# Masking the keys instead of the values in the state update of an mLSTM decode kernel

## The reference

```
ws = exp(src - m_new)                       # a weight for each token
decay = exp(b_last + m - m_new)
C_new = decay * C + einsum('bsh,bshv,bshk->bhvk', ws, vb, kb)
```

## Time and profile before

| | |
|---|---|
| median of 3 runs | 1560.38 us (1559.88 to 1560.7) |
| profiled execution, first to last instruction (span) | 1558.1 us |
| profiled execution, whole time | not on the page; the median of the runs is 2.3 us above the span |
| PE busy | 1529.1 us, 98% |
| DVE busy | 890.9 us, 57% |
| ACT busy | 659.0 us, 42% |

### The profile page before, as it was taken

How to read it: one execution, slowest core, us unless ns; L and a number is a source line. 1 busy time by engine, 2 the same in 40 slices (tenths; PEclk the granted TensorE clock), 3 DMA queues, 4 the chain that set the end, 5 groups by cost and what they waited for, 6 DMA issues and landing times.

```text
span 1558.1 us, 30694 instructions
## 1 busy us (share of the span) xinstructions
PE 1529.1 (98%) x11365; PEld 1497.8 (96%) x11365; DVE 890.9 (57%) x1522; ACT 659.0 (42%) x928; POOL 78.8 (5%) x142
## 2 busy tenths in 40 slices
PE   6999999999999999999999999999999999999996
PEld 5999999999999999999999999999999999999996
DVE  5655565554443447676666666676667644444443
ACT  5433333333333334454545454544544434343442
POOL 3000000000000000101000000101010000000000
PEclk9999999999999999999999999999999999999998
DMA  6674655556555554564747374747465555555543
GB/s 185 211 172 136 174 150 170 159 163 217 162 162 164 168 155 141 164 215 129 234 122 249 113 260 116 244 124 243 129 208 163 182 162 162 166 165 172 181 155 135
DMA packets 233137, 268.03 MB, mean 172 GB/s; under 512 B 8656, under 2 KB 221848, under 8 KB 232112
## 3 DMA queue, kind: packets, MB, share of 16 engines
q1 hardware_dynamic: 221472, 226.36, 48.5%
q0 software_dynamic: 11632, 41.22, 7.6%
HBM read 244.48 MB, written 23.06 MB: 172 GB/s over the span
## 4 chain that ended last, share of the span: by engine, by line
PE 92%; issue 5%; DVE 1%; DMA 1%; ACT 0%; POOL 0%; DVEq 0%; SPq 0%; POOLq 0%; ACTq 0%
PE ps L394 27%; PE ps L395 27%; PE ps L396 27%; PE ps L561 2%; PE ps L549 2%; PE ps L573 1%; PE ps L694 1%; PE ps L623 1%; PE ps L518 1%; DMA xt<-in_x_sample_dram 1%; PE ps L423 0%; DVE otok L1481 0%; PE ps L520 0%; PE ps L684 0%; PE ps L658 0%
## 5 line engine op out<-in xcount | busy, mean ns | idle before, releaser
L989 DVE TENSOR_TENSOR wlo<-raw,whi 128x1024 fp32r<-128x1024 f32 x416 | 508.2, 1224 | 577.8 <-ACT whi L746 574.7
L394 PE MATMUL ps<-xh,whi 128*128 128x288 f32 x2560 | 768.3, 300 | 0.0
L746 ACT ACTIVATE whi<-raw 128x1024 fp32r<-128x1024 f32 x416 | 440.2, 1059 | 766.5 <-PE ps L396 752.4
L396 PE MATMUL ps<-xh,wlo 128*128 128x288 f32 x2560 | 757.0, 296 | 0.0
L395 PE MATMUL ps<-xl,whi 128*128 128x288 f32 x2560 | 756.9, 296 | 0.0
L394 PEld LDWEIGHTS ps<-xh,whi 128*128 128x128 f32 x2560 | 482.0, 188 | 3.5 <-issue 1.2
L395 PEld LDWEIGHTS ps<-xl,whi 128*128 128x128 f32 x2560 | 482.5, 188 | 0.2
L396 PEld LDWEIGHTS ps<-xh,wlo 128*128 128x128 f32 x2560 | 481.9, 188 | 0.0
L394 PE MATMUL ps<-yh,whi 128*128 128x288 f32 x512 | 151.9, 297 | 0.0
L395 PE MATMUL ps<-yl,whi 128*128 128x288 f32 x512 | 151.4, 296 | 0.0
L396 PE MATMUL ps<-yh,wlo 128*128 128x288 f32 x512 | 151.3, 296 | 0.0
(11 more groups left out here) (308 smaller groups left out, 1146.0 us busy)
## 6 DMA issues: line engine op xcount, KB each, us to landing
raw<-in_w_in_dram SPq DMA_DIRECT2D x320, 512.0 KB, 3.7
raw<-in_w_pb_dram SPq DMA_DIRECT2D x32, 512.0 KB, 3.5
Cin<-in_state_mlstm_C_dram POOLq DMA_DIRECT2D x16, 1024.0 KB, 8.5
out_dram<-Cin POOLq DMA_DIRECT2D x16, 1024.0 KB, 6.2
raw<-in_w_pa_dram SPq DMA_DIRECT2D x32, 512.0 KB, 3.5
raw<-in_w_out_dram SPq DMA_DIRECT2D x32, 512.0 KB, 3.5
xt<-in_x_prompt_dram SPq DMA_DIRECT2D x2, 1024.0 KB, 6.1
out_dram<-cpo POOLq DMA_DIRECT2D x8, 256.0 KB, 2.4
```

The costliest lines, as they stand in the source:

```text
L394: nc.tensor.matmul(out, whi[:, c, kk, cols], mh_[:, k, :], start=(k == 0), stop=False)
L396: last = nc.tensor.matmul(out, wlo[:, c, kk, cols], mh_[:, k, :], start=False, stop=(k == KT - 1))
L746: nc.scalar.activation(whi[:, c], raw[:, c], ACT.Copy).then_inc(hi_ready, 1)
L989: nc.vector.tensor_tensor(wlo[:, c], raw[:, c], whi[:, c].bitcast(F32), ALU.subtract).then_inc(lo_ready, 1)
```

## The change

The mask goes to the other operand. `of_sequence` writes masked keys, `km[:, b % 4]`, from `kst`; `vst` is the stationary operand for all sequences, every second column for each half. `new_states(h, q)` handles the pair of sequences 2q and 2q+1: two matmuls, one for each half of the values, each with the masked keys of both sequences as 512 moving columns, into bank 2 for the first half and bank 3 for the second. Each pair uses the same two banks, so from q = 1 on it waits until both `add_state` of the pair before are done; it also waits for both masks at its start. `cs_mm` counts pairs instead of sequences. `add_state` reads its two halves from two banks. Bank 5 is no longer used by the update, and the wait for it ahead of line 694 goes.

```diff
--- before.py
+++ after.py
@@ -51,7 +51,7 @@
 Y_PARTS = ([(P, 0, slice(c, c + D // 4)) for c in (0, D // 4)] + [(P, 0, slice(D // 2, D))]
            + [(P, 1, slice(c, c + D // 2)) for c in (0, D // 2)] + [(S, 2, slice(0, D))])
 LO = 32
-NEW_BANK = (2, 3, 5)
+NEW_BANK = 2
 EPS = 1e-6
 MASKED = -30000.0
 NEVER = -3.0e38
@@ -205,7 +205,7 @@
     qk = a("qk", [P, 4, T])
 
 
-    vm = nc.alloc_sbuf_tensor_at("vm", [P, 4, XPW], F32R, offset=a.at)[:, :, 4:4 + DH]
+    km = nc.alloc_sbuf_tensor_at("km", [P, 4, XPW], F32R, offset=a.at)[:, :, 4:4 + DH]
     xp = a("xp", [P, 4, XPW])
     kv4 = a("kv4", [P, 2, 2, P])
     hb = a("hb", [P, 3, DH])
@@ -289,9 +289,9 @@
     kt_t, kt_ev, kvs_t, kvs_ev, vt_t, vt_ev, num_mm, den_step, r_set, sq_set, var_set, rs_set, f_set = (
         sem(n) for n in ("kt_t", "kt_ev", "kvs_t", "kvs_ev", "vt_t", "vt_ev", "num_mm", "den_step", "r_set",
                          "sq_set", "var_set", "rs_set", "f_set"))
-    h_set, ht_t, z_set, gate_set, yf_set, ya_hi, cp_mm, cp_ev, nn_ev, vm_set, cs_mm, cs_ev = (
+    h_set, ht_t, z_set, gate_set, yf_set, ya_hi, cp_mm, cp_ev, nn_ev, km_set, cs_mm, cs_ev = (
         sem(n) for n in ("h_set", "ht_t", "z_set", "gate_set", "yf_set", "ya_hi", "cp_mm", "cp_ev",
-                         "nn_ev", "vm_set", "cs_mm", "cs_ev"))
+                         "nn_ev", "km_set", "cs_mm", "cs_ev"))
     q_step, ct_lo, lo_rows = sem("q_step"), sem("ct_lo"), sem("lo_rows")
     inter_mm = sem("inter_mm")
     ya_lo, st_lo, kv4_set = sem("ya_lo"), sem("st_lo"), sem("kv4_set")
@@ -564,14 +564,14 @@
                                             skip_group_check=True)
             last.then_inc(inter_mm, 1)
 
-        def new_state(h, b):
-
-            pe.wait_ge(vm_set, 8 * h + b + 1)
-            if b >= 3:
-                pe.wait_ge(cs_ev, 8 * h + b - 2)
+        def new_states(h, q):
+
+            pe.wait_ge(km_set, 8 * h + 2 * q + 2)
+            if q >= 1:
+                pe.wait_ge(cs_ev, 8 * h + 2 * q)
             for vh in range(2):
-                last = nc.tensor.matmul(ps[:, NEW_BANK[b % 3], DH * vh:DH * vh + DH],
-                                        vm[:, b % 4, vh::2], kst[:], start=True, stop=True)
+                last = nc.tensor.matmul(ps[:, NEW_BANK + vh, :], vst[:, vh::2],
+                                        km[:, 2 * (q % 2):2 * (q % 2) + 2, :], start=True, stop=True)
             last.then_inc(cs_mm, 1)
 
         with pe.Fori(0, HEADS) as h:
@@ -659,8 +659,7 @@
                                                 vz[:, j, P * t:P * t + P], ident[:])
                     last.then_inc(vt_t, 1)
                     pe.wait_ge(slot_free[1], H_USE[1] + 2 + 2 * h)
-                    for b in range(2):
-                        new_state(h, b)
+                    new_states(h, 0)
                 if c == 1:
 
                     pe.wait_ge(lo_rows, h + 1)
@@ -672,11 +671,9 @@
 
                     nc.tensor.matmul(ps[0:S, X4, 0:DH + 1], W[0:2 * S, 384:416], vtok_h[0:2 * S, 2, :],
                                      start=False, stop=True, skip_group_check=True).then_inc(num_mm, 1)
-                    for b in range(2, 4):
-                        new_state(h, b)
+                    new_states(h, 1)
                 if c == 2:
-                    for b in range(4, 6):
-                        new_state(h, b)
+                    new_states(h, 2)
                 if c == 3:
                     pe.wait_ge(h_set, h + 1)
                     for j in range(2):
@@ -685,10 +682,7 @@
                         last = pe.transpose(ps[:, X6 + j, TP:T], hb[0:S, 2, P * j:P * j + P],
                                             ident[0:S, 0:S])
                     last.then_inc(ht_t, 1)
-                    for b in range(6, NB):
-                        new_state(h, b)
-
-                    pe.wait_ge(cs_ev, 8 * h + 6)
+                    new_states(h, 3)
                     for vh in range(2):
                         for t in range(2):
                             last = nc.tensor.matmul(ps[:, X5, DH * vh:DH * vh + DH], vtok_h[:, t, vh:DH:2],
@@ -1257,14 +1251,14 @@
 
         def of_sequence(h, b):
             if b >= 4:
-                dve.wait_ge(cs_mm, 8 * h + b - 3)
-            nc.vector.tensor_scalar(vm[:, b % 4, :], vst[:].bitcast(F32), mask8[:, b:b + 1], None,
-                                    ALU.mult).then_inc(vm_set, 1)
+                dve.wait_ge(cs_mm, 4 * h + b // 2 - 1)
+            nc.vector.tensor_scalar(km[:, b % 4, :], kst[:].bitcast(F32), mask8[:, b:b + 1], None,
+                                    ALU.mult).then_inc(km_set, 1)
 
         def add_state(h, b):
-            dve.wait_ge(cs_mm, 8 * h + b + 1)
+            dve.wait_ge(cs_mm, 4 * h + b // 2 + 1)
             nc.vector.scalar_tensor_tensor(Cin[:, b], Cin[:, b], dec_bc[:, ds(8 * h + b, 1)],
-                                           ps[:, NEW_BANK[b % 3], :].rearrange("p (v k) -> p v k", v=2),
+                                           ps[:, NEW_BANK:NEW_BANK + 2, DH * (b % 2):DH * (b % 2) + DH],
                                            ALU.mult, ALU.add).then_inc(cs_ev, 1)
 
         with dve.Fori(0, HEADS) as h:
```

## The result

The changed kernel takes 1564.12 us (median of 10 runs, 1563.27 to 1564.63) against 1559.97 for the one before (10 runs, 1559.41 to 1560.7): ratio 1.0026, 95% interval 1.0017 to 1.0035. It is 4.15 us slower. Forecast: 1563.4, range 1559.3 to 1565.0, that is +3.0 us with bounds of +1.2 and +3.8 for the two holds (a hold is a place where PE stands idle at a wait). The time lies in the range; the increase is just over the upper bound of its own sum. On the forecast's own base of 1560.4 it would be 1564.5, in the range too.

What follows compares the result with a forecast made beforehand. PE, 98% busy, was taken to bound the kernel. Per head 0.21 + 0.21 - 0.04 = 0.38 us, over 8 heads +3.0, took the span from 1558.1 to 1561.1; with 2.3 more, 1563.4 us, range 1559.3 to 1565.0.

Steps and rivals of the forecast that it cites:

- Pair 0's hold: At each head's first pair, PE waits for both masks instead of one: 0.21 us later, 0.10 to 0.25.
- Pair 2's hold: At the third pair, PE waits for the add_state of sequence 3: 0.21 us late, 0.10 to 0.25.
- pair 1's gain: At the second pair no wait holds; it gains 0.04 us, which is only waited at pair 2.
- The wide matmul: In new_states, two matmuls of 512 columns replace four of 256: 443 ns a pair for 480, 37 ns less.
- p: Pitch of one wide fp32r matmul on PE: 216 to 227 ns, taken as 222.
- d + l: At a hold, DVE's end to weight load (0.10 us) plus load to first column (0.11 us).
- DVE, roles, banks: Masked keys, swapped operands and add_state reading two PSUM banks were claimed to cost nothing.
- Nothing takes the delay back: After each hold, PE waits nowhere for something that doesn't itself start from PE, so the delay stays.
- (a): Rival: weights go in ahead of the held matmul, so l vanishes from both holds; +1.3 us, 1561.7; chance 0.12.
- (b): Rival: only one hold binds, pair 0 or pair 2 alone; +0.7 to +1.0 us, 1561.3; chance 0.10.
- (c): Rival: neither hold binds, -1.2 us, 1559.2, or a far cheaper wide matmul; chance 0.09, of which 0.03 the latter.
- (d): Rival: a wide fp32r matmul takes as long as plain fp32, 432 ns; +13 us, 1577; chance with other slowing 0.06.

Runs made afterwards that it cites:

- e3: The changed kernel with pair 0 as four matmuls of 256 columns, each sequence waiting for its own mask alone: 1562.22 us against 1559.78, ratio 1.0016.
- e1: The changed kernel, same waits and banks, but each pair as four matmuls of 256 columns instead of two of 512: 1564.3 us against 1559.78, ratio 1.0030.
- e4: The changed kernel with the add_state of sequence 3 right behind that of sequence 2, all pairs wide: 1561.81 us against 1559.78, ratio 1.0013.
- e2: The kernel before with only the roles swapped, masked keys moving and values stationary, one sequence at a time: 1560.09 us against 1559.78, ratio 1.0003.
- e5: The changed kernel with the edits of e3 and e4 together: 1560.09 us against 1559.85, ratio 0.9999.
- e7: e6 with each wide matmul issued twice, 64 more in all: 1574.42 us, 14.37 over e6.
- e6: The changed kernel, all pairs wide, add_state 3 early, pair 0 moved behind the first six matmuls of chunk 1: 1560.05 us against 1559.85, ratio 1.0001.
- e10: The kernel before with only the v transposes moved to bank 6, not waiting for st_lo: 1559.83 us against 1559.93, ratio 1.0001.

## Why the prediction was right, step by step

- **Pair 0's hold:** forecast 0.21 (0.10 to 0.25), measured 0.26. Shown by e3, which takes it away, and e1, which keeps it without the wide matmul. The distance from mask to load (d) was 0.11 for the 0.10 taken. The prediction took the old load at 1048.22 for one that ran on without waiting. It stood 1048.22 - (1047.76 + 0.35) = 0.11 behind the end of the first mask, the distance of a load that a wait just released, and so it does in all eight heads (0.12). The new load stands at the same distance behind the second mask. So the hold is the 0.27 between two masks less the 0.01 that the wide pair gains, whatever d and l are.
- **Pair 2's hold:** forecast 0.21, measured 0.28 behind L394 of pair 1; with pair 1's gain, 0.27. d was 0.12. The load was 0.17 ahead of the end of `add_state` 3 and is 0.12 behind it: 0.29, less 0.01. Shown by e4. As forecast, pair 1's 0.01 is only waited there.
- **The wide matmul:** the mis-sized term. Forecast p 222 ns (216 to 227), measured 235 in the chain and 232 over seven heads, outside the bounds. It is in every pair: 2 x 0.013 at each hold, and pairs 1 and 3 gain 0.01 in place of 0.04. For the upper bound I had taken the 13 ns beside the 107 of 256 columns as a cost of each instruction. By the chain most of it grows with the columns: 120 ns for 256 is 0.47 ns a column, a chunk's (1058.20 - 1054.54 - 0.48)/24 = 133 ns for 288 is 0.46, and 235 for 512 is 0.46. So joining matmuls saves only about 0.01 us a pair (0.47 for 0.48 in the chain; 0.04 a head between e1 and the changed kernel).
- **d + l:** with p = 0.235 the stretch from mask to L394, 1052.52 - 1051.82 = 0.70, leaves 0.23 for d + l, 0.21 taken. All the sizes are off to the same side; the sum, 0.38 a head, came out at 0.52, 3.0 us at 4.2.
- **DVE, roles, banks:** costed at nothing. e2 shows about 0.3 us for the roles, the 744 ns of `add_state` for the two banks.
- **Nothing takes the delay back:** right; e5 and the 0.53 a head.
- **Rivals:** (a) weights ahead of the held matmul: against it the after trace, the loads at 1051.93 and 1061.59 come 0.11 and 0.12 behind the releaser and not before. The pulling of weight loads ahead of matmuls in flight that the Trainium skill's page "TensorE: Matmul & The Clock Gate" (Step-by-step: what each phase is for) states does not reach over a wait here. (b) one hold: both are there. (c) neither, or a far cheaper wide matmul: e7. (d) a wide matmul as slow as plain fp32: e7.
- **The chances:** slower by over 0.2% had 0.38, same 0.59; the measured 0.26% is over that bound, though its interval begins at 0.17%, below it. The forecast stood 0.1 us under the bound, and the mis-sized terms decided the side.

## What to carry to other kernels

When matmuls are joined into wider ones, look at what the wide one must wait for: the last input of all its parts, and all the room that it writes. Here each join gained 0.01 us and two of four cost over 0.25 us on a PE that is busy 98% of the time. And before the number of instructions is counted as a saving, take the cost for each column at two widths: if it is the same, there is nothing per instruction to save. Holds hang on small margins: the old loads came 0.16 (pair 0) and 0.17 us (pair 2) before the end of the input that the new ones wait for, and that decided this change. Moving the producer's step (e4) or the consumer (e6) by one place gave it back.

## What the runs showed of the hardware

- A fp32r matmul of 512 columns takes 235 ns at the granted 2.4 GHz in a stream (e7's chain), and not the 512/2.4 = 213 of its columns; one of the two records of a plain fp32 matmul of 256 columns takes 216. Why fp32r costs more for each column stays open.
- The load of a held matmul starts 0.12 us behind the end of the DVE instruction that releases it, in all eight heads within 0.01 (pairs 0 and 2 after, e10's first mask; L658 before). The first column is an estimated 0.12 later, from the 0.23 for d + l above: a hold costs about 0.23 us beyond the releaser's end even when it is missed by little.
- A wait that ends just as the engine arrives leaves no idle time in the views. It shows by its distance: pair 0's load of the kernel before stands 0.12 behind the end of the first mask in every head. That it was released there is read from the distance; no run moved the first mask alone.
- A DVE read that spans two banks of PSUM took as long as one in a single bank, 744 ns for 512 fp32 elements (`add_state` before and after).
